# Recurrence: VectorE's other work of each level placed between the masks and the subtractions

## The reference, cut to what matters

```python
def stream(h, S0):                        # context first, then the latent tokens from its state
    ...
    w = heads(jnp.exp(-jnp.exp(logw)))    # decay, one for each direction
    a = heads(jax.nn.sigmoid(...))
    kk = heads(k * k_k)
    kk = kk / jnp.maximum(jnp.linalg.norm(kk, axis=-1, keepdims=True), 1e-12)
    kt = heads(k)[None] * (1 + (a - 1) * heads(k_a))
    S_f, y_f = _rwkv_scan(S0[0], (r, w[0], kk, kk * a[0], kt[0], v), False)
    S_b, y_b = _rwkv_scan(S0[1], (r, w[1], kk, kk * a[1], kt[1], v), True)
    return (S_f, S_b), (y_f + y_b, r, kt, v, g)

def readout(y, r, kt, v, g, dtype):
    ...                                   # mean and variance over each head
    yn = (y - mu) * rsqrt(var + eps) * ln_g + ln_b
    bonus = sum over directions and channels of (r * kt * r_k), times v
    return ((yn + bonus) * g) @ w_o
```

## The kernel before

| group, level | work in the slot | instructions |
|---|---|---|
| 0, 1 and 0, 2 | `weigh_bonus` (L1967 to L1973) | 3 and 3 of 128x512 |
| 0, 3 | `unit_keys` part 1 (L1935 to L1937) | 3 of 128x768 |
| 0, 4 | `unit_keys` part 2 (L1940 to L1942) | 2 small, 1 of 128x768 |
| 1, 1 to 1, 4 | `read_out` parts 1 to 4 (L2056 to L2075) | 3 or 2 of 128x512 and a small one; part 3 has 4 |
| 1, 2 also | `factors` for z = 0 (L1948 to L1950) | 3 of 128x768 |
| 2, 1 | `scale` for z = 0 (L1957 to L1960) | 1 of 128x512, 3 of 128x768 |
| 2, 2 | `factors` for z = 1 | 3 of 128x768 |
| 2, 4 | `scale` for z = 1 | 4 as above |

## Time and profile before

### The profile page before, as it was taken

The page is one execution under the profiler, slowest core; times in us unless marked ns, Lnnn a source line. Parts: engine busy times, 40 slices in busy tenths (PEclk is TensorE's granted clock), DMA queues, the critical chain, the costliest instruction groups (busy, mean ns, idle before and its releaser), DMA issues. The chain is left out here.

```text
span 5166.3 us, 86103 instructions
## 1 busy us (share of the span) xinstructions
PE 4709.0 (91%) x36862; PEld 2597.0 (50%) x36862; DVE 1442.5 (28%) x3612; ACT 1176.0 (23%) x2575; POOL 336.1 (7%) x544
## 2 busy tenths in 40 slices
PE   8999999989999899996999997996888888869998
PEld 6775444444444346753444443445666666634333
DVE  1131110010001213533222224134455555431222
ACT  2131111011101322423222221032333333312111
POOL 0000000000002013312000000021000000010000
PEclk9999999999999898997999998996677888779999
DMA  3243121222122113422777773242000000029998
GB/s 129 76 154 123 49 78 57 82 77 82 65 81 77 34 56 104 123 73 98 290 290 287 287 290 111 88 154 76 27 27 27 27 27 8 3 94 372 408 407 344
DMA packets 253798, 679.82 MB, mean 132 GB/s; under 512 B 23568, under 2 KB 60288, under 8 KB 253168
## 3 DMA queue, kind: packets, MB, share of 16 engines
q1 hardware_dynamic: 225824, 601.94, 31.5%
q0 software_dynamic: 27600, 72.37, 4.8%
HBM read 644.76 MB, written 26.74 MB: 130 GB/s over the span
## 5 line engine op out<-in xcount | busy, mean ns | idle before, releaser
L2174 PE MATMUL bank<-ring,arena 128*128 128x512 f32 x2592 | 1126.3, 595 | 20.4 <-DVE arena L1904 11.3
L2174 PEld LDWEIGHTS bank<-ring,arena 128*128 128x128 f32 x2592 | 559.2, 217 | 564.2 <-issue 475.7
L2542 PE MATMUL bank<-ring,arena 128*64 128x512 f32 x2048 | 471.9, 600 | 10.7 <-DMA ring<-in_moe_w 8.0
L2174 PE MATMUL bank<-arena,ring 128*128 128x512 f32 x1024 | 440.8, 592 | 1.9 <-ACT arena L1148 1.2
L1849 DVE TENSOR_TENSOR arena<-arena,bank 128x512 f32<-128x512 f32 x300 | 187.2, 683 | 649.5 <-PE bank L2515 580.5
L2174 PEld LDWEIGHTS bank<-arena,ring 128*128 128x128 f32 x1024 | 194.5, 190 | 245.8 <-issue 243.3
L2542 PEld LDWEIGHTS bank<-ring,arena 128*64 128x64 f32 x2048 | 140.0, 137 | 314.3 <-issue 311.2
L2568 PE MATMUL bank<-ring,arena 128*64 128x512 f32 x1024 | 232.0, 600 | 1.6 <-ACT arena L1368 1.6
L2345 PE MATMUL bank<-ring,arena 128*128 128x512 f32 x512 | 219.9, 592 | 0.0
L2771 PE MATMUL bank<-ident,arena 128*128 128x128 f32 x480 | 129.6, 361 | 71.1 <-ACT arena L1472 20.9
L1361 ACT ACTIVATE arena<-bank 64x512 f32<-64x512 f32 x64 | 37.7, 588 | 665.5 <-PE bank L2542 665.5
(11 more groups left out here) (403 smaller groups left out, 5925.5 us busy)
## 6 DMA issues: line engine op xcount, KB each, us to landing
ring<-in_moe_w SPq DMA_DIRECT2D x768, 512.0 KB, 7.7
ring<-in_w_in SPq DMA_DIRECT2D x21, 2048.0 KB, 7.8
ring<-in_ada_w SPq DMA_DIRECT2D x12, 2048.0 KB, 8.0
ring<-in_ada_w SPq DMA_DIRECT2D x24, 1024.0 KB, 5.3
ring<-in_w_up SPq DMA_DIRECT2D x8, 2048.0 KB, 8.1
ring<-in_w_down SPq DMA_DIRECT2D x8, 2048.0 KB, 8.0
ring<-in_na_w_qkv SPq DMA_DIRECT2D x6, 2048.0 KB, 8.0
ring<-in_w_in SPq DMA_DIRECT2D x8, 1024.0 KB, 6.3
```

Of the source, the lines that this page charges most:

```text
L2174: ins = mm(ps[:, 0:ncol], lhs(k), rhs(k), start=(k == 0 and first), stop=(k == nk - 1))
L2542: ins = mm(ps, x_chosen[:, b, k, 0:CAP_L], w[x][:, n * W:(n + 1) * W], start=(k == 0), stop=(k == KD - 1))
```

## The change

DVE's list in a level was: masks, `scan_u`, subtractions, `scan_state`, slot of other work. It is now: masks, `scan_u`, slot of other work, subtractions, `scan_state`. Nothing is added or removed, and the lists of PE, ACT, POOL and the DMA queue (SP) are the same as before. In the new file the subtraction's line is 2120.

```diff
@@ -2094,16 +2094,6 @@
                     if beside:
                         scan_u(*beside)
-                    for z in range(0 if last else 2):
-                        ps = two_banks(full(dve, "rw_join", p, g, z, lv), CH).rearrange("p h (j a b) -> p j h a b", j=RW_TILES, b=1 << lv)
-                        T = halves(inv[z], lv, z)
-                        if lv == 1:
-                            taken(dve, "rw_a", p, g, z)
-                        else:
-                            taken(dve, "rw_join", p, g, z, lv - 1)
-                        free(V.tensor_tensor(T, T, ps, ALU.subtract), "rw_join", p, g, z, lv)
-                    if beside:
-                        scan_state(*beside)
                     if g == 0 and lv <= 2:
                         weigh_bonus(p, lv)
...
                     if (g, lv) == (2, 4) and goes_on:
                         scale(p + 1, 1)
+                    for z in range(0 if last else 2):
+                        ...
+                        free(V.tensor_tensor(T, T, ps, ALU.subtract), "rw_join", p, g, z, lv)
+                    if beside:
+                        scan_state(*beside)
```

More of the change, by code:

```diff
@@ L2122, in _ @@
                         scale(p + 1, 1)
+                    for z in range(0 if last else 2):
+                        ps = two_banks(full(dve, "rw_join", p, g, z, lv), CH).rearrange("p h (j a b) -> p j h a b", j=RW_TILES, b=1 << lv)
+                        T = halves(inv[z], lv, z)
+                        if lv == 1:
+                            taken(dve, "rw_a", p, g, z)
+                        else:
+                            taken(dve, "rw_join", p, g, z, lv - 1)
+                        free(V.tensor_tensor(T, T, ps, ALU.subtract), "rw_join", p, g, z, lv)
+                    if beside:
+                        scan_state(*beside)
                 for z in range(2):
```

## The result

| | before | changed |
|---|---|---|
| median of 4 runs | 5204.99 us | 5347.39 us (5335.65 to 5352.68) |
| ratio | | 1.0268 (95% interval 1.0226 to 1.0311) |
| profiled execution, its span | 5166.3 us | 5341.6 us |
| from the first mask to the last (the recurrence) | 960.9 us | 1093.8 us |
| granted clock there, of full speed | 0.75 | 0.66 |

The forecast was 5275 us, +80 us; measured are +142 us between the medians. The two spans differ by 175 us, of which 133 lie in the recurrence. The first mask is already 45 us later in the changed kernel (3580.6 against 3535.8 us), behind code that is alike in both.

The account below looks back on a forecast made before the run. The recurrence was taken as bound by a chain of hand-overs, neither PE nor DVE full. Lateness 94 less 28.9 us of mask waits gave +65, clock +15: 5195 + 80 = 5275 us, range 5215 to 5320.

Parts of the forecast that it names:

- The mechanism and its place: In the recurrence, masks would come sooner, but subtractions and states behind the slot later, making PE's products late.
- The terms behind `scan_u`: Per level, PE's next product starts after slot plus 1.55 us (states) or 0.25 us (subtraction); lateness 94 us in all.
- tail: DVE's work behind the slot until PE's product can start: 1.55 us for banks 0 and 1, 0.25 us for a transpose.
- the step of +65: PE's waits in the recurrence: 94 us of lateness less 28.9 us of mask waits removed, +65 us, bounds 40 and 90.
- the term for PE's clock: In the recurrence, 0.04 less granted clock from added PE idling, +15 us, bounds 0 and 50 us.
- one of the signs: Forecast wrong if the recurrence's granted clock moves by more than 0.04 from 0.75, or L2764 waits for ACT, not DVE.
- group 0, level 2 should look as before: There the y products and ACT's copy cover the slot, 1.6 us of cover remaining, so no lateness.
- two windows of 120 us: Clock price in the recurrence: 1886 matmuls at 0.70, 1984 at 0.82, 5% more, or 50 us for 0.12 of clock.
- the clock falls as well: Rival: gaps in group 2 keep the clock at 1.2 GHz for most of the recurrence, 65 + 50 = 115, 5310 us; chance 0.15.
- lateness shrinks at half clock: Argument against the 5310 us rival: in the recurrence at half clock, PE itself takes longer, so lateness is smaller.
- the mask waits go with nothing in their place: Rival: PE's y products, ACT's copies and transposes cover the slot, saving the full 28.9 us, 5166 us; chance 0.05.
- the lateness is covered or cancelled: Rival: half clock, cancelled mask waits or better overlapping tails in the recurrence leave +0 to +50 us, middle 5220; chance 0.20.

Follow-up runs that it names:

- early_plain_levels: Slot ahead of the subtractions only in group 0 levels 2, 3, 4 and group 1 levels 2, 3, against the kernel before: 5160.00 us, ratio 0.9991.
- slot_between_subtractions_and_states: Against the kernel before, slot moved between the subtractions and the states in every level: 5323.66 us, ratio 1.0267.

## Why the prediction was wrong

**What held.** The mechanism and its place. The mask waits went, as forecast. The terms behind `scan_u` came out close. For pair 1, time from the end of `scan_u` to PE's next product, forecast and measured:

| group, level | forecast (slot + tail) | measured |
|---|---|---|
| 2, 1 | 3.29 + 1.55 = 4.84 us | 4.67 |
| 2, 2 | 2.8 + 1.55 = 4.35 | 4.31 |
| 2, 4 | 4.84 | 4.67 |
| 0, 1 | 3.65 | 3.64 |
| 1, 1 | 3.85 | 3.84 |
| 1, 2 | 4.59 | 4.62 |
| 0, 2 (covered) | 3.95 as before | 3.94 |

PE's waits for the states, the subtractions and the masks at the lines of the forecast (L2764, L2667, L2771, L2654 and L2813) sum to 51.7 us before and 113.3 us in the changed kernel, +62 us where the forecast had +65. All its waits in the recurrence, for any engine, sum to 155.6 and 206.3 us, +51 us, since those for ACT and the idle time without a named cause became shorter. A part of the lateness does not show as a wait, since PE at half clock is itself later at the products in question: L2667 in group 2, level 2 waits 0.81 us in pair 1 while it starts at the forecast time. So the step of +65 stands: it was 14 us too high as a sum, and inside its bounds of 40 and 90.

**What failed** is the last step, the term for PE's clock: "I take 0.04 less clock, +15 us". Two things in it were too small.

- *The fall.* The clock went from 0.75 to 0.66, not to 0.71, and a move of more than 0.04 was one of the signs that the prediction had named for being wrong. I thought mainly of group 2; in the changed kernel the clock is at 1.2 GHz also in group 0, levels 2 and 3, in all seven pairs with a step there, where no wait was added (the windows of pair 5 above). Counted from one `scan_u` to the next and summed over the pairs, PE's busy time rose by 46 us in group 2, by 32 us in group 0 and by 4 us in group 1, so "group 0, level 2 should look as before" was right for the order of the waits and wrong for the time.
- *The price.* I read it from two windows of 120 us in the earlier trace rows, as 5% for 0.12. The windows do not hold the same work: the first has the `sums` (L2654) of one pair in it, the second those of two. The windows of pair 5 hold the same level: 7.42 us at 1.2 GHz and 4.69 us at 2.4 GHz, 58% more. A clock of 0.75 is half of the time at 1.2 GHz and 0.66 is 68%, 18 points more. With 58% as the price of a level and a stretch of 961 us, that is at most 961 x 0.18 x 0.58 = 100 us; other parts of a pair depend less on the clock. Two whole pairs of the kernel before, each from `scan_u` of group 1, level 1 to the same one a pair later (pair 1, then pair 5), show a price that I could have read:

```profile
3700.14:3830.71 130.57, 110.50 (x2000) 85.34 (x1992) 68.99 (x185) 43.97 (x109) 7.91 (x10) 0.70 0.10 27
4202.27:4322.56 120.29, 98.49 (x1996) 76.14 (x1992) 68.46 (x185) 43.60 (x109) 2.30 (x3) 0.82 0.03 9
```

That is 12% more busy time for 0.12 of clock, and so some 70 us for the 0.09 by which the clock fell (9% of 804 us, an estimate). Measured is PE's busy time for the same matmuls, 804.05 to 886.41 us, **+82 us** where the term had +15.

So 51 us of wait and 82 us of slower PE make the 133 us. Both bounds of the term were named (0 and 50 us), and the true value lay above the upper one. The rival "the clock falls as well" (5310 us, chance 0.15) had the right mechanism and the wrong price; with 82 instead of 50 us it gives 5195 + 65 + 82 = 5342 us, and 5347.39 was measured. That this comes so close is partly luck: the waits were 51 us and not 65, and the median of before had become 5204.99 us, 10 above the 5195. Its argument that lateness shrinks at half clock was right for the waits and beside the point for the time.

Of the two statements of the Trainium skill ("TensorE: Matmul & The Clock Gate"), the trace bears out the one on what is actually happening, that the throttled state is the default and activity releases it: with 30 more products per pair the clock went from 0.66 to 0.78. By that rule the prediction had put the term towards its upper bound of 50 us, and it was 82. The one on loop structure, that a VectorE copy out of PSUM between products leaves the clock alone, does not cover this case: here products wait 1 to 3 us for VectorE, and the clock fell from 0.75 to 0.66.

**The other rivals.** That the mask waits go with nothing in their place is refuted by L2764's waits. That the lateness is covered or cancelled holds for the levels of early_plain_levels, taken together (0.9991), and not for the other six (1.0247).

**What stays open.** Why the clock fell where it did (in group 0, levels 2 and 3, for one) is not shown, nor why in the kernel before it was low in these levels in pairs 1 to 3 and high in pairs 4 to 7: the runs change the number of gaps in whole groups, not single ones. The sum of the waits alone does not set the clock either: early_plain_levels had 7 us more of them than before (162.6 against 155.6) and a clock of 0.78. The 45 us by which the first mask was later in the profiled execution of the changed kernel are not explained by anything in this change, and the four runs of before alone spread over 41 us. The filler changes PE's work and its gaps together; that it works through the clock rests on the clock of the windows and on the busy time that fell with more instructions.

## What to carry to other kernels

Before other work is moved ahead of a hand-over, count for each place what stands behind it and when its reader comes, with buffers that have to come free (here banks 0 and 1) as well as data; a gap closed on one side of the slot can open on the other. Work that nobody waits for soon belongs where the engine is idle and nothing of the chain stands behind it (here level 5), not merely further from the wait that one sees. And where PE's granted clock is between its two levels, a new gap on PE can cost more than its length: price it from the same piece of work at either level, not from windows that average over different work.

## What the runs showed of the hardware

- The same 15324 matmuls took PE 774 us of busy time at a granted clock of 0.78 (early_plain_levels) and 888 us at 0.66 (slot_between_subtractions_and_states); with 468 matmul instructions more and a clock of 0.87 it was 777 us.
- One level of the recurrence took 4.69 us at 2.4 GHz and 7.42 us at 1.2 GHz, both in the same execution of the kernel before.
- A microsecond of added wait on PE went with about 2.6 us of time in the change (51 us of waits, 133 us) and about 1.9 us in group 2 alone (34 and 66 us). In the levels of early_plain_levels, 7 us more of waits cost nothing that the runs can tell.
- Useless products in PE's gaps gave back half of a slowdown (1.0268 to 1.0133), and on the kernel that had smaller gaps they neither cost nor gave anything (1.0012, interval 0.9994 to 1.0029).
